# Feed-forward weights split for TensorE: earlier request of the down unit, weight sums moved ahead of a split, sums of h on GpSimd

## What is computed

```python
for l in range(DEPTH):                       # DEPTH = 2
    x = layer_norm(ALPHA*x + 0.5*swiglu(x, ffn1_w_gate[l], ffn1_w_up[l], ffn1_w_down[l]), ...)
    h = x @ w_in[l]                          # q, k, v of 8 stick-breaking and 8 chunked heads
    ...                                      # both attentions, RMS norm of each head
    x = layer_norm(ALPHA*x + mixed @ w_out[l], ...)
    x = layer_norm(ALPHA*x + 0.5*swiglu(x, ffn2_w_gate[l], ffn2_w_up[l], ffn2_w_down[l]), ...)

def swiglu(x, w_gate, w_up, w_down):         # inner width F = 2816
    return (silu(x @ w_gate) * (x @ w_up)) @ w_down
```

## Time and profile before

| | us |
|---|---|
| median of three runs | 1081.44 |
| lowest, highest | 1073.92, 1085.91 |
| the profiled execution | 1086.01 |
| its span, first to last instruction | 1084.4 |
| TensorE busy in it | 1019.4 |
| VectorE, ScalarE, GpSimd busy | 815.7, 571.1, 31.0 |

### The profile page before, as it was taken

The page is one execution under the profiler, slowest core; times in us unless marked ns, Lnnn a source line. Parts: engine busy times, 40 slices in busy tenths (PEclk is TensorE's granted clock), DMA queues, the critical chain, the costliest instruction groups (busy, mean ns, idle before and its releaser), DMA issues.

```text
span 1084.4 us, 18717 instructions
## 1 busy us (share of the span) xinstructions
PE 1019.4 (94%) x7020; PEld 931.4 (86%) x7020; DVE 815.7 (75%) x934; ACT 571.1 (53%) x616; POOL 31.0 (3%) x54
## 2 busy tenths in 40 slices
PE   6899999999999899989988999999999998999998
PEld 6788888799988798989877888988999887898897
DVE  4878876945787878786957878778457977878778
ACT  4445444457685445544444545445586755445444
POOL 2100000001100000000010000000010000000000
PEclk9899999999999899999988999999999998999999
DMA  8554554463326354635444454644523354454542
GB/s 331 212 187 164 191 182 168 155 218 132 118 78 228 123 199 157 225 134 215 156 170 182 155 195 155 220 166 156 208 105 117 111 201 167 183 191 157 193 163 71
DMA packets 34088, 185.33 MB, mean 171 GB/s; under 512 B 3824, under 2 KB 3824, under 8 KB 18928
## 3 DMA queue, kind: packets, MB, share of 16 engines
q1 hardware_dynamic: 32400, 174.60, 44.7%
q0 software_dynamic: 1488, 9.45, 2.3%
q10 hardware_dynamic: 144, 0.52, 0.1%
HBM read 183.51 MB, written 1.05 MB: 170 GB/s over the span
## 4 chain that ended last, share of the span: by engine, by line
PE 44%; DVE 27%; DMA 16%; issue 11%; DVEq 1%; ACT 0%; SPq 0%
DMA raw<-stream 16%; PE bank L1014 11%; PE bank L1016 11%; PE bank L1015 11%; PE bank L1112 8%; DVE w_lo L696 7%; DVE w_lo L703 5%; DVE stick_t L686 4%; DVE w_lo L678 3%; DVE soft_t L822 2%; PE bank L1076 2%; DVE h_lo L844 1%; PE bank L1069 1%; DVE stick_t L685 1%; DVE soft_t L830 1%
## 5 line engine op out<-in xcount | busy, mean ns | idle before, releaser
L1014 PE MATMUL bank<-xT_hi,w_hi 128*128 128x256 f32 x1568 | 448.6, 286 | 30.0 <-DVE soft_t L822 27.0
L1015 PE MATMUL bank<-xT_lo,w_hi 128*128 128x256 f32 x1568 | 444.5, 284 | 0.0
L1016 PE MATMUL bank<-xT_hi,w_lo 128*128 128x256 f32 x1568 | 444.4, 283 | 0.0
L678 DVE TENSOR_TENSOR w_lo<-raw,w_hi 128x2048 fp32r<-128x2048 f32 x122 | 278.2, 2288 | 139.0 <-ACT w_hi L406 139.0
L1014 PEld LDWEIGHTS bank<-xT_hi,w_hi 128*128 128x128 f32 x1568 | 301.5, 192 | 44.9 <-issue 42.9
L1015 PEld LDWEIGHTS bank<-xT_lo,w_hi 128*128 128x128 f32 x1568 | 301.4, 192 | 1.9
L1016 PEld LDWEIGHTS bank<-xT_hi,w_lo 128*128 128x128 f32 x1568 | 301.3, 192 | 0.0
L406 ACT ACTIVATE w_hi<-raw 128x2048 fp32r<-128x2048 f32 x122 | 232.7, 1911 | 59.9 <-PE bank L1016 55.7
L1014 PE MATMUL bank<-w_hi,h_hi 128*128 128x512 f32 x284 | 115.9, 408 | 18.2 <-DVE h_lo L844 18.2
L1015 PE MATMUL bank<-w_lo,h_hi 128*128 128x512 f32 x284 | 115.2, 406 | 0.0
L1016 PE MATMUL bank<-w_hi,h_lo 128*128 128x512 f32 x284 | 113.8, 401 | 0.0
(11 more groups left out here) (138 smaller groups left out, 1185.4 us busy)
## 6 DMA issues: line engine op xcount, KB each, us to landing
raw<-stream SPq DMA_DIRECT2D x110, 1024.0 KB, 4.9
raw<-stream SPq DMA_DIRECT2D x110, 512.0 KB, 4.6
lnp<-ln_gb POOLq DMA_DIRECT2D x6, 1024.0 KB, 5.0
band<-rel_band POOLq DMA_DIRECT2D x2, 1024.0 KB, 8.8
xn<-x POOLq DMA_DIRECT2D x1, 1024.0 KB, 7.6
out<-xn SPq DMA_DIRECT2D x4, 256.0 KB, 2.0
qT<-xT SPq DMA_DIRECT2D x1, 512.0 KB, 4.9
qT<-xT ACTq DMA_DIRECT2D x1, 512.0 KB, 5.1
```

The costliest lines, as they stand in the source:

```text
L678: nc.vector.tensor_tensor(w_lo[:, at(slot)], raw[:, slot, :], w_hi[:, at(slot)].bitcast(F32), ALU.subtract).then_inc(lo_ready, 1)
L1014: nc.tensor.matmul(o, w[0], x[0], start=start, stop=False, skip_group_check=again)
L1015: nc.tensor.matmul(o, w[0], x[1], start=False, stop=False, skip_group_check=again)
L1016: return nc.tensor.matmul(o, w[1], x[0], start=False, stop=stop, skip_group_check=again)
```

## The change

- **SP.** `ffn_loads` issues the loads of a phase in an order of its own. In step j: gate unit 3j+5; then, once the pure part's low half (`lo_part`) and the three weight sums (`wsum_done`) of down unit j are done, down unit 3j+7 (`fetch`, which has no wait of its own); then up unit 3j+6. Before, the down unit came after the up unit, when the low half of the old one was complete.
- **GpSimd.** `h_sums` moves there, with three instructions (256, 256 and 128 elements a partition), before the load of the next norm's weights. `wait_alone` waits for `hf_done`.
- **ScalarE.** h_hi of the next step now stands at the end of a step, after the up unit's split, with a wait for M7 and for the sums.
- **VectorE.** The order of a step becomes: last parts low, weight sums, gate unit's low half, pure part, differences, gating, up unit's low half, h_lo. At a phase's start the weight sums stand ahead of the gating, and h_lo ahead of the differences and the up unit's split. The sums for the last two pieces, which nothing read, fall away.
- **End of a phase.** Two of the eight additions of `gather` move from its first to its second part.

TensorE's order is the same; one wait's count changes. Cut to the core:

```diff
+            def ffn_loads(l, f):
+                first = l * UNITS + FFN_BASE[f]
+                load(0, first + 3)
+                load(1, first + 4)
+                with sp.Fori(0, SF) as j:
+                    load(2, first + 3 * j + 5)
+                    sp.wait_ge(lo_part, 2 * strassen(l, f, j) + 1)
+                    sp.wait_ge(wsum_done, 3 * strassen(l, f, j) + 3)
+                    fetch(1, first + 3 * j + 7)
+                    load(0, first + 3 * j + 6)
+                load(2, first + FFN_UNITS - 1)
...
+            def h_sums(l, f):
+                with pool.Fori(0, SF) as j:
+                    wait_alone(hf_done, it(l, f, j) + 1)
+                    nc.gpsimd.tensor_tensor(hs[:, 2:4, :], hs[:, 7:9, :], hs[:, 0:2, :], ALU.add)
+                    nc.gpsimd.tensor_tensor(hs[:, 4:6, :], hs[:, 0:9:8, :], hs[:, 1:8:6, :], ALU.subtract)
+                    nc.gpsimd.tensor_tensor(hs[:, 6, :], hs[:, 7, :], hs[:, 1, :], ALU.add).then_inc(hsum_done, 1)
...
                 nc.gpsimd.memset(band[0:64, :, 192:256], NEG).then_inc(band_ready, 1)
+                h_sums(l, 0)
                 load_lnp(l, 1)
...
                 load_lnp(l, 2)
+                h_sums(l, 1)
...
-                split_parts_hi(l, f, 0)
+                split_pure_hi()
+                def high_h(j):
+                    act.wait_ge(hsum_done, strassen(l, f, j) + 1)
+                    nc.scalar.activation(h_hi[:, :, :], hs[:, 1:8, :], ACT.Copy).then_inc(hhi_done, 1)
+                high_h(0)
+                split_differences_hi(l, f, 0)
                 def step(j):
                     act.wait_ge(unit_used, used(l, base + 3 * j + 1))
-                    act.wait_ge(hsum_done, (2 * l + f) * (SF + 1) + j + 1)
-                    nc.scalar.activation(h_hi[:, :, :], hs[:, 1:8, :], ACT.Copy).then_inc(hhi_done, 1)
                     split_last_parts_hi(l, f, j)
...
-                    split_parts_hi(l, f, j + 1)
+                    split_pure_hi()
+                    split_differences_hi(l, f, j + 1)
                     split_hi(l, base + 3 * j + 6, 0, first[0] + 2 + j)
+                    act.wait_ge(unit_used, used(l, base + 3 * j + 4))
+                    high_h(j + 1)
...
                 split_lo(l, base + 2, 2)
+                weight_sums(l, f, 0, FILLED[base + 1] + 1)
                 gated(0, 1, bank[7], first=True)
-                h_sums(0)
-                split_lo(l, base + 3, 0)
-                weight_sums(l, f, 0, FILLED[base + 1] + 1)
-                split_parts_lo(l, f, 0)
+                split_pure_lo(l, f, 0)
+                low_h(0)
+                split_differences_lo(l, f, 0)
+                split_lo(l, base + 3, 0)
+                with dve.Fori(0, SF - 1) as j:
                     split_last_parts_lo(l, base + 3 * j + 4)
+                    weight_sums(l, f, j + 1, FILLED[base + 1] + 2 + j)
                     split_lo(l, base + 3 * j + 5, 2)
+                    split_pure_lo(l, f, j + 1)
+                    split_differences_lo(l, f, j + 1)
                     gated(j + 1, 3 * j + 3, bank[0])
                     split_lo(l, base + 3 * j + 6, 0)
+                    low_h(j + 1)
```

More of the change, by code:

```diff
@@ L298, in load, with fetch @@
                 sp.wait_ge(lo_ready, n + (4 - back))
-                n = n if source is None else source
+                fetch(slot, n if source is None else source)
+            def fetch(slot, n):
                 if slot == 0:
@@ L308, in _ @@
             with sp.Fori(0, DEPTH) as l:
-                with sp.Fori(0, (FFN_UNITS + WIN_UNITS) // 3) as i:
+                for s in range(3):
+                    load(s, l * UNITS + s)
+                ffn_loads(l, 0)
+                with sp.Fori(0, WIN_UNITS // 3) as i:
                     for s in range(3):
-                        load(s, l * UNITS + i * 3 + s)
+                        load(s, l * UNITS + ATT0 + i * 3 + s)
                 for a in range(WOUT_UNITS):
@@ L316, in _ @@
                     load(s, l * UNITS + FFN_BASE[1] + s, back=2 if s == 1 else 3)
-                with sp.Fori(1, FFN_UNITS // 3) as i:
-                    for s in range(3):
-                        load(s, l * UNITS + FFN_BASE[1] + i * 3 + s)
+                ffn_loads(l, 1)
             load(0, DEPTH * UNITS, source=DEPTH * UNITS - 1)
@@ L406, in split_hi, with split_pure_hi, split_differences_hi @@
                 nc.scalar.activation(w_hi[:, at(slot)], raw[:, slot, :], ACT.Copy).then_inc(hi_ready, 1)
-            def split_parts_hi(l, f, j):
+            def split_pure_hi():
                 nc.scalar.activation(w_hi[:, at(1, seven(0, 2))], raw[:, 1, 512:1536], ACT.Copy).then_inc(hi_part, 1)
+            def split_differences_hi(l, f, j):
                 act.wait_ge(wsum_done, 3 * strassen(l, f, j) + 1)
@@ L689, in weight_sums, with split_pure_lo, split_differences_lo @@
                                         ALU.add).then_inc(wsum_done, 1)
[L691 to L697, removed]
+            def split_pure_lo(l, f, j):
+                c = at(1, seven(0, 2))
+                dve.wait_ge(hi_part, 2 * strassen(l, f, j) + 1)
+                nc.vector.tensor_tensor(w_lo[:, c], raw[:, 1, 512:1536], w_hi[:, c].bitcast(F32),
+                                        ALU.subtract).then_inc(lo_part, 1)
+            def split_differences_lo(l, f, j):
+                c = at(1, seven(2, 2))
+                dve.wait_ge(hi_part, 2 * strassen(l, f, j) + 2)
+                nc.vector.tensor_tensor(w_lo[:, c], wsum[:, 0:1024], w_hi[:, c].bitcast(F32),
+                                        ALU.subtract).then_inc(lo_part, 1)
             def split_last_parts_lo(l, rel):
@@ L803, in gather @@
                     add(3, 1, 0, 4, ALU.subtract, first=True)
+                    add(3, 0, 0, 4, ALU.subtract, after=1)
+                else:
                     add(4, 0, 1, 3, ALU.add, first=True)
                     add(4, 1, 1, 3, ALU.add, first=True)
[L806 to L809, removed]
+                    add(2, 1, 1, 2, ALU.subtract, after=5)
+                    add(5, 0, 0, 1, ALU.add, after=3)
                     add(5, 1, 1, 1, ALU.add, after=6)
@@ L824, in gated, with low_h @@
                                                    op1=ALU.mult).then_inc(hf_done, 1)
[L826 to L832, removed]
                 split_lo(l, base + 1, 1)
                 split_lo(l, base + 2, 2)
+                weight_sums(l, f, 0, FILLED[base + 1] + 1)
                 gated(0, 1, bank[7], first=True)
-                h_sums(0)
-                split_lo(l, base + 3, 0)
-                weight_sums(l, f, 0, FILLED[base + 1] + 1)
-                split_parts_lo(l, f, 0)
-                def step(j):
+                split_pure_lo(l, f, 0)
+                def low_h(j):
                     dve.wait_ge(hhi_done, it(l, f, j) + 1)
@@ L845, in step @@
                                             ALU.subtract).then_inc(hlo_done, 1)
+                low_h(0)
+                split_differences_lo(l, f, 0)
+                split_lo(l, base + 3, 0)
+                with dve.Fori(0, SF - 1) as j:
                     split_last_parts_lo(l, base + 3 * j + 4)
+                    weight_sums(l, f, j + 1, FILLED[base + 1] + 2 + j)
                     split_lo(l, base + 3 * j + 5, 2)
-                def next_h(j):
+                    split_pure_lo(l, f, j + 1)
+                    split_differences_lo(l, f, j + 1)
                     gated(j + 1, 3 * j + 3, bank[0])
-                    h_sums(j + 1)
                     split_lo(l, base + 3 * j + 6, 0)
[L854 to L860, removed]
+                    low_h(j + 1)
+                split_last_parts_lo(l, base + 3 * SF + 1)
+                split_lo(l, base + 3 * SF + 2, 2)
+                gated(SF, 3 * SF, bank[0])
+                split_lo(l, base + 3 * SF + 3, 0)
                 gather(l, f, 0)
@@ L1164, in ffn @@
                 gate(SF)
-                pe.wait_ge(m_read, (2 * l + f) * 8 + 5)
+                pe.wait_ge(m_read, (2 * l + f) * 8 + 3)
                 up(SF, bank[4])
```

## The result

| | before | changed |
|---|---|---|
| median, us | 1083.68 (4 runs, 1073.92 to 1087.22) | 1045.22 (4 runs, 1044.47 to 1047.35) |
| the profiled execution | 1086.01 | 1044.47 |
| its span | 1084.4 | 1042.8 |

The changed kernel takes 0.966 of the time, with a 95% interval of 0.960 to 0.973. The forecast was 1050.0 us.

The account below looks back on a forecast made before the run. TensorE was taken as the bound, its gaps caused by the late down unit and weight sums. Steps 28.2 + starts 10.4 - late h_lo 1.3 - first phase 5.9 = 31.4 us off 1081.4: 1050.0 us, range 1039 to 1070.

Parts of the forecast that it names:

- The bound and its cause: Feed-forward phases: TensorE's gaps come from the raw down unit asked for too late, with the weight sums behind it.
- The steps: Four windows of seven steps, gate 1 to gate 8: from 492.48 us to 28 steps at 16.58, gaining 28.2 us.
- late h_lo: One h_lo per phase 0.3 us late, as VectorE and GpSimd start the step with no lead: minus 1.3 us.
- X: Time of GpSimd's three sums of h per step: 1.7 us taken as nearest, bounds 1.1 and 5.0.
- the doubled slope: Estimate for GpSimd's sums if two inputs are fetched one after the other: 0.64 + 0.64 + 0.40 = 1.7 us.
- GpSimd in series with VectorE: After a gating, GpSimd's sums can be put off by the up unit's VectorE split (2.28 us), not by more.
- The loop to watch: Steady step, gating to gating: 14.56 + X, 16.3 us with X 1.7; TensorE's 16.58 bounds up to X = 2.0.
- Starts of the last three phases: Next gate some 14.2 us after gate 0's end, not 18.04, 17.53 and 17.54: 10.4 us gained.
- Start of the first phase: GpSimd stands at its wait for the band, so gate 1 starts at 52.5, not 46.64: minus 5.9 us.
- The sum: Whole kernel: 28.2 + 10.4 - 1.3 - 5.9 = 31.4 us gained, 1050.0 us against the median of 1081.4.

Follow-up runs that it names:

- experiments three and four: Three: changed kernel with the down unit's old late request, 1214.86 us, ratio 1.12. Four: kernel before with only the new order of loads, 1060.49 us, ratio 0.980.
- the extra additions: Changed kernel with two more 256-element additions on GpSimd per step, ahead of the three sums, results unused: 1094.01 us, ratio 1.013 to the kernel before.
- the memset: Changed kernel with an unused 1536-element memset on GpSimd per step, ahead of the three sums: 1066.68 us, ratio 0.988 to the kernel before.
- both kernels with extra work: Changed kernel with two more GpSimd additions per step (1094.01 us), and changed kernel with a GpSimd memset per step (1066.68 us).
- the reordering: Changed kernel with h sums on VectorE and each phase's second gating ahead of the pure and difference splits: 1026.44 us, ratio 0.950 to the kernel before.

## Why the prediction was right, point by point

**The bound and its cause: right.** The gaps were the late weight sums. With the request early and the sums ahead, they went (experiments three and four).

**The steps: right, and mis-sized by the cost of a stop.** 31.9 us came back (492.48 to 460.55) where the prediction had 28.2, less 1.3 for late h_lo. It took 16.58 us for a step's need from a step that had a wait in it. A step without one takes 16.32. The trace's gap is counted from the modelled end of the last product, 0.39 us after its start, while in an unbroken run the next product starts 0.22 after it (82.61 and 82.83): 0.17 us of the difference. The rest is the first product after a stop, which is shown with 0.38 us and not 0.28. So the 28 stops cost 28 x 0.26 = 7.3 us more than their gaps. Against it stand 3.6 us that weren't in the sum: the four stretches together are that much longer than 28 steps of 16.32. Of these, 2.7 are the two gates at the low clock (115.81 and 115.83 against 114.46); the prediction named such a price, 1 to 2 us each, without counting it. The late h_lo in the second step, 1.3 us, didn't show: no stretch after gate 1 has a wait. 28.2 + 7.3 - 3.6 is 31.9.

**X: right.** The sums took 0.71, 0.71 and 0.44 us, from 32.69 to 34.49: X = 1.80, as against 1.7 from the doubled slope of one-input rows. The Trainium skill's factor of 1.96 (GPSIMD Engine Reference, Performance versus the Vector engine), measured there at 2048 elements, would have made it 2.2, by an estimate; here the ratio is 1.86 over 1.12, 1.66.

**GpSimd in series with VectorE: right.** It was put off by the one split, not by more (82.99 to 85.81), and the extra additions cost their whole length (1.39 us a step for 1.40 us). The Trainium skill's rule (SBUF — State Buffer, Who interferes with whom) says that a GpSimd instruction that only writes isn't concerned; the memset bears that out.

**The loop to watch: wrong step, without harm to the number.** The prediction let TensorE be the bound up to X = 2.0, by the loop from gating to gating, and summed no loop by way of h_lo and product 5. The tighter one runs from the end of the up products: 0.2 to ScalarE, high half 1.92, VectorE's split 2.29, what GpSimd has left after it 1.0, h_hi 0.95, h_lo 1.09, and hand-overs of 0.35, together 7.8. TensorE gives it 7.81 (80.77 to 88.58): the products up to M7 and the next gate. So the kernel stood at the edge, not 0.3 us from it (16.58 less 16.3). There was luck in the loop's terms as well: VectorE's split of the up unit starts 0.80 us after the gating, since it waits for ScalarE, which the sum didn't have, and the first sum of h runs in that time. From the end of the gating to h_hi it is 4.13 us (82.12 to 86.25) against 4.21 in the sum, made of other parts. The memset, costing 0.70 where 0 to 0.3 was expected, showed it; so did h_lo as the releaser in both kernels with extra work.

**Starts of the last three phases: right.** End of gate 0 to gate 1 takes 13.86, 13.53 and 14.14 us; 14.2 was forecast. Gained 4.2 + 4.0 + 3.4 = 11.6, forecast 10.4. The waits of about 2 us at the second gate were there (1.88, 1.89, 2.04), from VectorE's backlog of 13 us, as the reordering showed. Product 5 waits 0.66, 0.33 and 0.78 us there and 8.12 in the first phase; 1 and 10 were forecast.

**Start of the first phase: right in kind, too dear.** 3.3 us were lost (46.64 to 49.98) where 5.9 were forecast. The band landed at 32.00 and not at 34.48, and the operation behind it took 0.24 with VectorE idle. Why the band was there earlier wasn't tried; GpSimd's own requests stood 0.8 us earlier in this trace (22.41, not 23.2), and the up unit's load, which before fell into the band's transfer at 27.58, now comes at 40.10; on the other hand the early request of the down unit, at 28.98, now falls into it. The prediction saw the loss but counted it to the change as a whole; it is the price of the sums' move to GpSimd only: with them on VectorE gate 1 starts at 44.76.

**The sum.** 31.9 + 11.6 - 3.3 = 40.2 of the 41.6 us between the spans; the other 1.4 lie outside these stretches. Forecast 31.4: 5.0 too little in the steps, 1.2 at the starts, 2.6 in the first phase. That the forecast of 1050.0 came within 5 us is in part luck: the gaps were read from an execution of 1086.0 and taken off a median of 1081.4. Against the profiled execution the same sum gave 1054.6, 10 us over the 1044.47 that the changed kernel's profiled execution took. What the prediction didn't ask is what each edit is worth by itself: the move of the sums to GpSimd, which it treated as part of the gain, is worth minus 12 us.

## What to carry to other kernels

When a transfer is waited for only briefly, look at what has been put ahead of the wait to cover it: the early request by itself was worth 21 us, about what the trace said (of 27.0 us of waits for the gating 6.1 are left), but it also permits a reordering worth another 27, which without it loses 134. Work moved to GpSimd isn't off VectorE's path where, as here, both have two inputs in SBUF: it stands in series with it, and if its result goes back through two more engines, the loop grows by the whole trip. Here that cost nothing in the steady steps, where TensorE stayed the bound with nothing to spare, and 10 us at the starts of the phases, 3 of them the wait for the band; on VectorE, which had room, the sums were cheaper. Count slack on each loop that closes through the bounding engine, not only on the one that was tight before.

## What the runs showed of the hardware

- A stop of TensorE costs about 0.25 us beyond the gap that the trace shows (16.57 us of work in a step with a stop, 16.32 in one without).
- After waits of almost the same length the granted clock fell in some cases and not in others. After 1.88 us at 363.80 gate 1 ran in 5.88 us at a clock of 1.00; after 1.89 at 560.04 it took 7.33, with the clock at 0.77 over it, that is in part at the 1.2 GHz level. In the kernel before, 2.11 us at 63.12 had the effect (second row) and 1.95 at 1017.34 had not. Each costs 1.5 us. The runs don't tell what decides it.

```profile
879.30:885.18 5.88, 5.88 (x36) 5.88 (x37) 2.89 (x3) 2.33 (x2) 3.44 (x3) 0.71 0.99 372
65.23:72.56 7.33, 7.33 (x49) 7.33 (x49) 5.58 (x7) 2.33 (x2) 0.00 (x0) 0.77 0.40 132
```

The first row is the first 5.88 us of the changed kernel's gate after 2.04 us of waiting, at a low clock too.

- GpSimd's read of a 128x256 pair lasted 2.82 us behind a VectorE split and 0.71 alone; a memset of 128x1536 took 1.39 us beside the split, and the split its usual 2.29.
- A GpSimd operation that was held didn't get in between VectorE instructions that followed each other without a pause. With the early request alone, the 8-element operation on the gains lasted 8.83 us, across seven of them, until VectorE's last one ended at 41.78:

```profile
33.05 8.83 POOL L397 TENSOR_SCALAR mixg<-mixg 128x8 f32<-128x8 f32 x1 [8.74 <-DMA band<-rel_band]
40.57 1.21 DVE L712 TENSOR_TENSOR w_lo<-stick_t,w_hi 128x1024 fp32r<-128x1024 f32 x1
```

In the changed kernel, with VectorE idle, it took 0.24. So what saves the sums of h is that VectorE has one split before them and then has to wait.
